# A hybrid decoder layer on one core: the last post-norm cut into column halves and token tiles, and ticks moved in its mixers

## The reference

```python
f = swiglu(rms_norm(x, ffn1_pre_g), ffn1_w_gate, ffn1_w_up, ffn1_w_down)     # 1024 -> 2816 -> 1024
x = x + 0.5 * rms_norm(f, ffn1_post_g)
proj = rms_norm(x, mix_pre_g) @ w_in
qa, ka, va, za, aa, ba, qb, kb, vb = split(proj)
o_a = gdn_mixer(...)        # gated DeltaNet, 4 heads x 128, conv of 4 taps, chunked delta rule
o_b = dilated_mixer(...)    # 8 heads x 64, three dilated windows with ALiBi, merged
x = x + rms_norm(concat([o_a, o_b]) @ w_out, mix_post_g)
x = x + rms_norm(memory_cross_attention(...), mem_post_g)                    # 4 heads, 256 keys
f = swiglu(rms_norm(x, ffn2_pre_g), ffn2_w_gate, ffn2_w_up, ffn2_w_down)
x = x + 0.5 * rms_norm(f, ffn2_post_g)
```

## Time and profile before

| | us |
|---|---|
| runs of before: median (lowest to highest of 3) | 2648.82 (2646.16 to 2651.15) |
| profiled execution | 2647.31 |
| its span, first to last instruction | 2645.6 |
| PE busy, of the span | 2554.3 (97%) |
| DVE busy | 1231.1 (47%) |
| ACT busy | 936.5 (35%) |
| POOL busy | 402.9 (15%) |
| mean granted clock of TensorE | 0.991 |

### The profile page before, as it was taken

One profiled execution on the slowest core, in us unless ns is written; L12 is line 12 of the kernel. 1 busy time (PEld: TensorE's weight loads), 2 busy tenths in 40 slices (PEclk: granted clock), 3 DMA queues, 4 the chain that ended last, 5 costly groups with the idle time before them and its releaser, 6 DMA issues.

```text
span 2645.6 us, 30948 instructions
## 1 busy us (share of the span) xinstructions
PE 2554.3 (97%) x12464; PEld 2090.3 (79%) x12464; DVE 1231.1 (47%) x1913; ACT 936.5 (35%) x1405; POOL 402.9 (15%) x491
## 2 busy tenths in 40 slices
PE   7999999999999999999999888999999999999996
PEld 7888887878888877778787777777787778888885
DVE  5463335644444444469444543333344435533333
ACT  5422224333332334445233322444443424322222
POOL 1460002001312210031213531000011002100001
PEclk9999999999999999999999999999999999999998
DMA  6553334334122233153233323222134234533331
GB/s 199 181 173 109 96 96 137 110 96 128 57 71 64 67 125 112 64 166 106 72 92 100 104 88 119 77 70 77 57 116 139 72 113 158 175 96 96 98 100 57
DMA packets 319199, 280.01 MB, mean 106 GB/s; under 512 B 12369, under 2 KB 266321, under 8 KB 318289
## 3 DMA queue, kind: packets, MB, share of 16 engines
q1 hardware_dynamic: 297856, 204.56, 26.0%
q0 software_dynamic: 20160, 73.46, 7.9%
q10 hardware_dynamic: 1040, 0.00, 0.0%
HBM read 248.63 MB, written 29.36 MB: 105 GB/s over the span
## 4 chain that ended last, share of the span: by engine, by line
PE 89%; DVE 5%; POOL 2%; issue 1%; DMA 1%; ACT 1%; SPq 0%; ACTq 0%; DVEq 0%; POOLq 0%
PE acc L907 16%; PE acc L909 15%; PE acc L908 15%; PE acc L932 9%; PE acc L934 9%; PE acc L933 9%; PE side L1113 3%; PE side L1139 2%; PE side L1049 1%; PE side L1066 1%; PE side L1128 1%; PE side L1191 1%; PE side L1223 1%; PE side L979 1%; POOL rs_pre L590 1%
## 5 line engine op out<-in xcount | busy, mean ns | idle before, releaser
L1775 DVE TENSOR_TENSOR w_lo<-w_raw,w_hi 128x1024 fp32r<-128x1024 f32 x384 | 488.2, 1272 | 542.5 <-ACT w_hi L1355 542.1
L1355 ACT ACTIVATE w_hi<-w_raw 128x1024 fp32r<-128x1024 f32 x384 | 405.2, 1055 | 513.5 <-PE acc L934 282.8
L907 PE MATMUL acc<-ha_hi,w_hi 128*128 128x512 f32 (+2 forms) x968 | 396.0, 409 | 2.8 <-DVE ha_lo L1948 1.1
L907 PE MATMUL acc<-hb_hi,w_hi 128*128 128x512 f32 (+1 forms) x968 | 377.6, 390 | 1.2 <-DVE w_lo L1775 1.2
L909 PE MATMUL acc<-hb_hi,w_lo 128*128 128x512 f32 (+1 forms) x968 | 376.7, 389 | 0.0
L908 PE MATMUL acc<-hb_lo,w_hi 128*128 128x512 f32 (+1 forms) x968 | 376.7, 389 | 0.0
L909 PE MATMUL acc<-ha_hi,w_lo 128*128 128x512 f32 (+2 forms) x968 | 374.2, 387 | 0.0
L908 PE MATMUL acc<-ha_lo,w_hi 128*128 128x512 f32 (+2 forms) x968 | 372.7, 385 | 0.0
L932 PE MATMUL acc<-w_hi,act_hi 128*128 128x512 f32 x704 | 285.4, 405 | 0.0
L934 PE MATMUL acc<-w_lo,act_hi 128*128 128x512 f32 x704 | 275.1, 391 | 0.0
L933 PE MATMUL acc<-w_hi,act_lo 128*128 128x512 f32 x704 | 274.4, 390 | 0.0
(11 more groups left out here) (329 smaller groups left out, 3472.4 us busy)
## 6 DMA issues: line engine op xcount, KB each, us to landing
w_raw<-in_ffn_w_gate SPq DMA_DIRECT2D x88, 512.0 KB, 3.7
w_raw<-in_ffn_w_up SPq DMA_DIRECT2D x88, 512.0 KB, 3.7
w_raw<-in_ffn_w_down SPq DMA_DIRECT2D x88, 512.0 KB, 3.3
w_raw<-in_w_in SPq DMA_DIRECT2D x56, 512.0 KB, 3.8
x_dram<-xbuf POOLq DMA_DIRECT2D x24, 512.0 KB, 3.0
xbuf<-x_dram POOLq DMA_DIRECT2D x24, 512.0 KB, 6.1
arena<-bias_dram POOLq DMA_DIRECT2D x16, 512.0 KB, 4.0
w_raw<-in_w_out SPq DMA_DIRECT2D x16, 512.0 KB, 3.3
```

The source lines that it names most:

```text
L907: pe.matmul(out, hi[:, k, 0:m], xh[:, k, 0:n], start=(k == 0), stop=False)
L1355: act.activation(w_hi[:, j % RING, :], w_raw[:, j % RING, :], ACT.Copy).then_inc(w_hi_ok, 1)
L1775: dve.tensor_tensor(w_lo[:, j % RING, :], w_raw[:, j % RING, :], w_hi[:, j % RING, :].bitcast(F32), ALU.subtract).then_inc(w_lo_ok, 1)
```

## The change

It has four parts.

- The last post-norm runs by column halves and token tiles. In the last down product the second column half goes tile by tile: for each token tile all four k blocks (12 matmuls), so that both weight granules are needed at its start and one tile is complete every 12 matmuls. ACT squares each half tile, POOL adds the two sums and makes the root with the factor 0.5 inside, DVE multiplies by the gain before the root is there (into `fg_end`, which lies where `hb` was), and one operation per tile adds it to x.
- An idle tick after step 3 of every delta-net chunk, and the idle tick between the second and the third `ab` step goes.
- Four `load` ticks instead of two, and the keys and values of the second pair of heads are loaded ahead of the second bias.
- Three ticks per granule instead of two in the last chunk of the FFN beside the first mixer, and in the down products of the two chunks beside the second. The first mixer now has 135 steps and the host work 138 ticks for them.

```diff
 def mixer_ticks(h):
-    t = [("ab", 0, 0), ("ab", 1, 0), ("idle", 0, 0), ("ab", 2, 0)]
-    t += [("chunk", l, k) for l in range(TT) for k in range(20)]
+    t = [("ab", k, 0) for k in range(3)]
+    for l in range(TT):
+        t += [("chunk", l, k) for k in range(4)] + [("idle", 0, 0)] + [("chunk", l, k) for k in range(4, 20)]
     t += [("last", k, 0) for k in range(3)]
-    t += [("load", k, 0) for k in range(2)]
+    t += [("load", k, 0) for k in range(4)]
...
                         bias_load(0)
+                        kv_load(h, 1)
                         bias_load(1)
-                        kv_load(h, 1)
...
-            for _ in norm(7, None):
-                pass
+            pool.dma_start(GROW[7][:], t[POST_GAIN[7]][0].partition_broadcast(P)).then_inc(grow_in, 16)
+
+            def end_store(k):
+                pool.wait_ge(post_x, 7 * TT + k + 1)
+                pool.dma_start(t["out"][0][(TT + k) * P:(TT + k + 1) * P, :], xbuf[:, k, :]).then_inc(x_stored[k], 16)
+
+            for k in range(TT):
+                n = 7 * TT + k
+                pool.wait_ge(end_ssq, TT + k + 1)
+                pool.tensor_tensor(ssq_post[:, n:n + 1], ssq_end[:, k:k + 1], ssq_end[:, TT + k:TT + k + 1], ALU.add).then_inc(end_sum, 1)
+                pool.wait_ge(end_sum, k + 1)
+
+                pool.tensor_scalar(rs_post[:, n:n + 1], ssq_post[:, n:n + 1], 4.0 / D, 4.0 * EPS, ALU.mult, ALU.add).then_inc(post_v, 1)
+                pool.wait_ge(post_v, n + 1)
+                pool.tensor_tensor(rs_post[:, n:n + 1], rs_post[:, n:n + 1], half_pow[:, 0:1], ALU.pow).then_inc(post_rs, 1)
+                if k:
+                    end_store(k - 1)
+            end_store(TT - 1)
...
             dn(0, 3)
-            ffn(0, ha, 1, 4, 2)
+            ffn(0, ha, 1, 3, 2)
+            ffn(0, ha, 3, 4, 3, 3)
...
-            ffn(1, ha, 0, 2, 3, 2)
+            ffn(1, ha, 0, 2, 3, 3)
...
+            for tt in range(TT):
+                bank_free(BANK[i] + tt)
+                out = A[(BANK[i] + tt) % NBANK][:]
+                ts = slice(tt * P, (tt + 1) * P)
+                for kk in range(4):
...
+            for ch in range(2):
+                for k in range(TT):
+                    act.wait_ge(acc_dve, EV[turn0 + (ch - 1) * TT + k][1])
...
+                    act.activation(junk_z[:, 0:TOK], res_cz[:, k, ch * TOK:(ch + 1) * TOK], ACT.Square,
+                                   accum_out=ssq_end[:, ch * TT + k:ch * TT + k + 1]).then_inc(end_ssq, 1)
...
+            def scaled(k, ch):
+                cs = slice(ch * TOK, (ch + 1) * TOK)
+                dve.wait_ge(acc_dve, EV[turn0 + (ch - 1) * TT + k][1])
+                dve.tensor_tensor(fg_end[:, k, cs], res_cz[:, k, cs], GROW[7][:, cs], ALU.mult).then_inc(end_fg, 1)
+
+            def new_x(k):
...
+                dve.scalar_tensor_tensor(out=xbuf[:, k, :], in0=fg_end[:, k, :], scalar=rs_post[:, n:n + 1], in1=xbuf[:, k, :],
+                                         op0=ALU.mult, op1=ALU.add).then_inc(post_x, 1)
+
+            for k in range(TT):
+                scaled(k, 0)
+            for k in range(TT):
+                dst = res_cz[:, k, TOK:]
...
+                dve.tensor_tensor(dst, A[(turn0 + k) % NBANK][:], dst, ALU.add).then_inc(acc_dve, 1)
+                scaled(k, 1)
+                if k:
+                    new_x(k - 1)
+            new_x(TT - 1)
```

More of the change, by code:

```diff
@@ L324, in hybrid_layer @@
         post_x = sem("post_x")
+        end_ssq = sem("end_ssq")
+        end_fg = sem("end_fg")
+        end_sum = sem("end_sum")
         conv_ok = sem("conv_ok")
@@ L1311, in _ @@
             job[0] = norm(6, None)
-            ffn(1, hb, 0, 4, 2)
+            ffn(1, hb, 0, 3, 2)
+            up(hb, CH[3], 2)
             finish()
-            for _ in norm(7, None):
-                pass
+            rgroup((act_hi, act_lo), 2, TT, 2, blk[0] - CH[3])
+            i = g[0]
+            g[0] += 2
+            pe.wait_ge(w_lo_ok, i + 2)
+            for tt in range(TT):
[3 more added lines that the diff above has]
+                for kk in range(4):
+                    hi, lo = rview(w_hi, i + kk // 2)[:, kk % 2, :], rview(w_lo, i + kk // 2)[:, kk % 2, :]
+                    pe.matmul(out, act_hi[:, kk, ts], hi, start=(kk == 0), stop=False)
+                    pe.matmul(out, act_lo[:, kk, ts], hi, start=False, stop=False)
+                    done = pe.matmul(out, act_hi[:, kk, ts], lo, start=False, stop=(kk == 3))
+                    if kk == 3 or (tt == 0 and kk == 1):
+                        done.then_inc(pe_done, 1)
             assert g[0] == NG
@@ L1411, in rgroup, with rows_to @@
                     pend[0] = lambda s=sub - 1, some=some: some(s)
-            def rows_to(res, n, sub, tiles=TT):
-                for ch in range(2):
+            def rows_to(res, n, sub, tiles=TT, halves=(0, 1)):
+                for ch in halves:
                     rgroup(n, tiles, sub, lambda tt, ch=ch: res[:, tt, ch * TOK:(ch + 1) * TOK])
@@ L1678, in _ @@
             dn(0, 3, oT)
-            ffn(1, 4, 2, oT)
+            ffn(1, 3, 2, oT)
+            ffn(3, 4, 3, oT, 3)
             finish()
@@ L1704, in _ @@
             job[0] = mix_job
-            ffn(0, 2, 3, oT, 2)
+            ffn(0, 2, 3, oT, 3)
             finish()
@@ L1725, in _ @@
             job[0] = norm(6, None)
-            ffn(0, 4, 2, res_cz)
+            ffn(0, 3, 2, res_cz)
+            up(0, CH[3], 2)
             finish()
+            rows_to(res_cz, 2, 2, halves=(0,))
             flush()
-            for _ in norm(7, None):
-                pass
+            turn0 = BANK[g[0]]
+            g[0] += 2
+            for ch in range(2):
+                for k in range(TT):
+                    act.wait_ge(acc_dve, EV[turn0 + (ch - 1) * TT + k][1])
+                    act.wait_ge(post_ssq, 7 * TT)
+                    if ch or k:
+                        act.wait_ge(end_ssq, ch * TT + k)
+                    act.activation(junk_z[:, 0:TOK], res_cz[:, k, ch * TOK:(ch + 1) * TOK], ACT.Square,
+                                   accum_out=ssq_end[:, ch * TT + k:ch * TT + k + 1]).then_inc(end_ssq, 1)
             assert g[0] == NG
@@ L1854, in up, with dn @@
                     pend[1] = lo
-            def dn(c, sub, res):
-                for ch in range(2):
+            def dn(c, sub, res, halves=(0, 1)):
+                for ch in halves:
                     def put(tt, turn, val, ch=ch):
@@ L2263, in _ @@
             job[0] = norm(6, None)
-            ffn(0, 4, 2, res_cz)
+            ffn(0, 3, 2, res_cz)
+            up(0, CH[3], 2)
             finish()
+            dn(3, 2, res_cz, halves=(0,))
             flush()
-            for _ in norm(7, None):
-                pass
+            turn0 = BANK[g[0]]
+            tile0 = TILE0[g[0] + 1]
+            g[0] += 2
+            dve.wait_ge(grow_in, 16 * 8)
+            def scaled(k, ch):
[3 more added lines that the diff above has]
+            def new_x(k):
+                n = 7 * TT + k
+                dve.wait_ge(x_in[k], 16 * x_turn(7, None))
+                dve.wait_ge(end_fg, TT + k + 1)
+                dve.wait_ge(post_rs, n + 1)
+                dve.scalar_tensor_tensor(out=xbuf[:, k, :], in0=fg_end[:, k, :], scalar=rs_post[:, n:n + 1], in1=xbuf[:, k, :],
[4 more added lines that the diff above has]
+                dst = res_cz[:, k, TOK:]
+                dve.wait_ge(acc_dve, EV[turn_of[1, k]][1])
+                dve.wait_ge(pe_done, tile0 + k + 1)
+                dve.tensor_tensor(dst, A[(turn0 + k) % NBANK][:], dst, ALU.add).then_inc(acc_dve, 1)
[3 more added lines that the diff above has]
+            new_x(TT - 1)
             assert g[0] == NG
```

2 lines of the change are left out of this document (added).

## The result

The changed kernel takes 2622.53 us, the median of four runs (2621.47 to 2625.31). The kernel before had 2648.22 in the runs beside it. The ratio is 0.9908, with a 95% interval of 0.9895 to 0.9920: 24.4 us faster, between 21 and 28 (the two medians lie 25.7 apart). The forecast was 20.3 us faster, 2628 us.

A forecast was written before the change was run, and what follows sets the result against it. PE, 89% of the chain, was taken to bound the kernel through its waits and the tail. Terms -6.5 - 8.6 - 3.4 + 4.0 - 5.1 - 3.2 + 2.5 = -20.3 us from 2648.8 gave 2628 us, range 2618 to 2638.

The forecast's parts named there:

- three named places: About 12 us tail after the last matmul, 7.01 us wait at first mixer's end, 7.36 us wait for attention's loads.
- Tail, -6.5: After the last matmul's end (P): last store issued at P+5.6 instead of P+12.15, 6.5 us less.
- The two bounds: Last store's issue after the last matmul's end P: P+4.7 without hindrance, P+6.6 with POOL's three operations each held 1 us.
- End of the first mixer, -8.6: First mixer's end: the 7.0 us wait for hb_lo and 1.6 us of lower clock go.
- Idle tick inside a chunk, -3.4: Step 4's transposes in delta-net chunks: all waits go, 3.4 us for the six later chunks.
- Idle tick taken from the start, +4.0: Mixers' starts: new waits for the decay's sums and longer step 2 waits, +2.5 us first mixer, +1.5 us second.
- Loads, -5.1: Before attention: second mixer's load wait falls 3.4 us, clock loss 0.8, first mixer's 0.9 us wait goes; swap counted nothing.
- Shifted alignment, -3.2: Second mixer beside kv_in and the norm: waits on DVE subtractions fall from 5.1 to 1.9 us; the finish changes nothing.
- Costs, +2.5: Attention at three ticks per granule costs 1 us in all; lower clock after new waits at mixers' starts, 1.5 together.
- new waits at alignments: Load wait stays near 7 us, kv_in keeps 5.1 us, clock falls at both starts: about 2637 us, 15 in 100.

The follow-up runs named there:

- ab_idle_h0: The changed kernel with the idle tick between the second and third decay steps put back in the first mixer alone (136 ticks of 138): 2624.52 us.
- last_two: The changed kernel with the last FFN chunk beside the first mixer back at two ticks a step: 2644.01 us.
- load_eight: The changed kernel with eight load ticks in the second mixer instead of four: 2618.62 us.
- tail_order: The changed kernel with the last two updates of the stream in the other order on DVE, stores likewise: 2625.38 us.
- dense: Changed kernel with rearranged idle and load ticks, plus three ticks in the last chunk but one beside the first mixer and idle ticks ahead of step 2: 2611.56 us.
- bias_first: The changed kernel with the second head's bias again issued ahead of the second keys and values: 2624.76 us.

## Why the prediction was right, and where it was off

The direction, the range and the three named places were right, for the reasons given; 4 us of 24 are missing from the sum. By its own steps, with the profiled execution's figures:

1. *Tail, -6.5.* -6.7 in the profile, -6.6 alone. POOL's first operation was held until the update beside it ended, as assumed (P+2.8), and the root was there at P+3.7 (P+3.9 forecast). The two bounds that the prediction sets beside this, P+4.7 and P+6.6, don't follow from its own figures, which give about P+4.5 and P+7.4; the sum uses neither.
2. *End of the first mixer, -8.6.* The 7.01 us wait is gone, and the lower clock behind it (3.12 us busy, 1.6 us): -8.6. Nothing else is late there, but the margin is under one tick (ab_idle_h0), and its worth depends on the other terms (last_two).
3. *Idle tick inside a chunk, -3.4.* All six waits are gone (3.4 us), and came back with 3.5 us when the ticks went. Taking them out costs 10 us, though, because of what they align.
4. *Idle tick from the start, +4.0.* This is the step that was mis-sized, in its waits by more than 4 us. The waits for the sums came as forecast (2.2 and 2.2 for 2.4 and 2.4), but step 2 waits 1.18 us in the first mixer, where 3.1 were forecast, and not at all in the second (2.0). In the executions of load_eight and tail_order it waits 2.83 and 1.38 us. What differs is the clock: where it falls right behind the first wait, PE's work up to step 2 takes longer and uses up the second wait. So term 4 is -0.3 us in waits (5.6 where the two starts had 5.9), and 5.1 us in clock, 3.6 more than the 1.5 that term 7 had for it. Together 4.8 against 5.5: the sum held while its two parts did not, and that is partly luck.
5. *Loads, -5.1.* -3.8: the 0.9 us wait is gone, and the other fell by 2.9 (forecast 3.4). The swap costs 1.3 us, so the ticks alone gave more than was forecast. The low clock behind it was not shorter (4.94 us busy before, 5.26 after).
6. *Shifted alignment, -3.2.* -1.1: the DVE subtraction waited for is now one instead of two, as said, but 3.24 us late, with 1.36 us more at a new place (L1024): 4.6 instead of 5.3. The finish gave 0.4; its 3.0 us wait for `ha_lo` replaces step 2's 3.73, as forecast (2.8).
7. *Costs, +2.5.* Attention at three ticks: no wait at all in the last chunk, nor in the chunk that dense adds (1 us forecast). The clock part is in point 4.

Not in the sum: 2.5 us of small waits that went because all later alignments changed (0.67 us on an evacuation at 875, 0.45 twice at 1118, 0.66 at 1927, 0.33 at 1472, and 0.7 of step 2's at 1486, less 0.79 new at 802). By the trace the waits fell by 17.9 us where the terms had 12.9.

A second thing was not in the sum. With the clock's 0.5 x 7.6 = 3.8 us taken off, PE's busy time is 3.4 us shorter than before. The rows around step 4 of the first chunk show why, before:

```profile
666.25 0.39 PE L909 MATMUL acc<-ha_hi,w_lo 128*128 128x512 f32 x1
668.45 0.66 PE L1038 MATMUL side<-ident,arena 128*128 128x128 f32 x4 [1.81 <-DVE arena L2039]
668.86 0.48 PE L907 MATMUL acc<-ha_hi,w_hi 128*128 128x512 f32 x1
```

and after:

```profile
669.48 0.39 PE L931 MATMUL acc<-ha_hi,w_lo 128*128 128x512 f32 x1
669.71 0.60 PE L1060 MATMUL side<-ident,arena 128*128 128x128 f32 x4
670.06 0.47 PE L929 MATMUL acc<-ha_hi,w_hi 128*128 128x512 f32 x1
```

From the end of the large matmul to the start of the next it is 668.86 - 666.64 = 2.22 us before, 0.41 more than the wait, and 670.06 - 669.87 = 0.19 after: the first transposes overlap the large matmul if nothing was waited for, and can't if something was. So a wait costs some 0.2 us more than its length. PE has 44 gaps of over 0.15 us before and 29 after, and 15 x 0.22 = 3.3 us, an estimate from this one place, is the 3.4 missing.

The terms as measured (the clock included, 0.2 us more behind the loads) add up to -6.7 - 8.6 - 3.4 + 4.8 - 3.6 - 1.1 = -18.6 us against the forecast's 20.3: terms 5 and 6 gave 3.6 us less, the others 1.9 more. The 2.5 us of small waits and the 3.4 of overlap, neither foreseen, make it 24.5, where the span says 24.2.

The rival "new waits at alignments" came in part: `kv_in` kept most of its wait and the clock fell at both starts. The load wait did not stay.

## What to carry to other kernels

In a schedule of ticks, what bounds a part is the number of ticks left at its end, and one change that adds host ticks pays for all that add list ticks. Undone one at a time, three parts (later idle ticks, load ticks, the last chunk's third tick) cost 10, 11 and 21.5 us, 43 together, and the tail alone gave 6.6, where the whole change was worth 24. So count the margin at the end (135 of 138 was enough, 136 was not) before a tick is added anywhere, and price a wait together with the clock behind it and the next wait downstream, since they replace each other. Each wait removed also gives back some 0.2 us of overlap.

## What was not expected of the hardware

The same wait in the same code is not always followed by the same clock. The 2.20 us wait at the second mixer's start is followed by 6.8 us at the lower clock in the changed kernel, by 3.4 us in ab_idle_h0, and by none in load_eight, tail_order and bias_first, whose programs are the same there. Over the nine traces with this start it is 6.8 us in two, 3.4 in three and none in four. Window of load_eight over the stretch that the changed kernel's clock was low in, and PE's two waits:

```profile
1273.20:1280.00 6.80, 4.71 (x32) 4.29 (x33) 4.30 (x17) 2.95 (x7) 0.00 (x0) 1.00 0.01 3
```

```profile
1275.29 0.40 PE L1175 MATMUL side<-sm,tri_u 128*128 128x16 f32 x2 [2.20 <-DVE sm L2169]
1285.09 1.09 PE L1018 MATMUL side<-ident,arena 128*128 128x128 f32 x8 [1.38 <-DVE arena L2079]
```

With the clock full the pair of waits costs 2.20 + 1.38 = 3.6 us; with it low for 3.4 us 2.20 + 0.95 + 1.7 = 4.9; with it low for 6.8 us 2.20 + 0 + 3.4 = 5.6. The mean over the nine is 4.5, so the changed kernel's profile shows the dearest case. At the first mixer's start the clock is low for 3.4 us in all eight traces without an idle tick there, behind the first wait in six and behind the second in load_eight and tail_order. This is a part of the spread between executions of one kernel (2621.47 to 2625.31 us here), and why a profile's single account can be 2 us off the median either way. What decides whether the clock falls behind such a wait was not found.
